# Expert sums: a 0/1 scatter in the rounded format, the gate moved to VectorE, the additions spread over four steps

## The chip, the cores and the metric

One core of one Trainium2 chip runs the whole program. The metric is the device time of one execution in microseconds; a kernel's time is the median of its runs.

## What is computed

The program runs two model blocks one after the other. The change touches only the last part of the second one, the mixture of eight experts over 256 tokens, each of 1024 features:

```python
def moe_swiglu(x, w_router, w_gu, w_down):
    logits = jnp.einsum('bsd,de->bse', x, w_router).astype(jnp.float32)
    top_logits, top_idx = lax.top_k(logits, TOP_K)
    top_gates = jax.nn.softmax(top_logits, axis=-1)
    gates = jnp.sum(jax.nn.one_hot(top_idx, N_EXPERTS, dtype=jnp.float32) * top_gates[..., None], axis=-2)
    gates = gates.astype(x.dtype)
    out = jnp.zeros_like(x)
    for e in range(N_EXPERTS):
        out = out + gates[..., e:e + 1] * swiglu_2(x, w_gu[e], w_down[e])
    return out
```

`swiglu_2` is `silu(x·Wg) * (x·Wu)`, then a product with `w_down`; the hidden width is 2816. All arrays are float32.

## The kernel before

**Products in the rounded format.** TensorE takes float32 operands in a rounded format (F32R). To keep the precision, every weight tile and every input is split into a rounded high part and a low part (the value less its high part), and three products are summed: high by high, high by low, low by high. ScalarE (ACT) writes the high parts (`w_hi`, `x_hi`, `k_hi`), VectorE (DVE) subtracts and writes the low parts (`w_lo`, `x_lo`, `k_lo`). There is one `w_hi`/`w_lo` buffer for each of three kinds of weight tile: front, back and down. So the high part of the next back tile can only be written after the matmuls of the current back tile have read it.

**An expert.** For each expert at most 128 of the 256 tokens are gathered by matmuls with a 0/1 matrix (`gather`, L1036) into `x_hi`/`x_lo`. They fill columns 0 to 127 of each 256-wide tile; columns 128 to 255 are free in this stage. The hidden width is walked in 11 steps of 256. Step p of TensorE does four things in this order: `front` (12 matmuls of 512 columns, the first half of the features, L1059), `turn_hidden` (two transposes of the hidden tile of step p-1, L1073), `back` (12 matmuls, the other half of the features, L1059), and `down` (12 matmuls that add the hidden tile of step p-1, times its part of `w_down`, to PS banks 0 and 1, L1084 to L1086). The down of an expert's last hidden tile therefore stands in step 0 of the next expert.

**The other engines in a step.** ACT: `hidden_high` (k_hi of the turned tile, L1535), `high("front")`, `silu` (L1531), `high("back")`, `high("down")` (all three at L1526). DVE: `hidden_low` (L2260, k_lo, which the down of that step waits for), `low("front")`, `hidden` (L2256, the product of gate and up), `low("back")`, `low("down")` (all three at L2250). Each of these waits for what it reads, and an engine takes them strictly in the order written. SyncE issues the weight loads, three tiles ahead of use for each kind.

**The sum of an expert.** When the last down of an expert is done, its output y (128 tokens by 1024) stands in banks 0 and 1. ACT copies it to `y_exp` in step 0 (`y_copy`, L1540). In step 1 TensorE, after its front, multiplies it by the scatter matrix: four float32 products of 512 columns into banks 2, 3, 7 and 5 (`scatter_sum`, L1094). It then clears banks 0 and 1 (`zero_sum`, L1049). The matrix holds the gate of each token, and zeros; DVE makes it in `make_picks` (L2238), TensorE turns it (`turn_scatter`), ACT copies it (`scatter_copy`, L1519). DVE adds the four banks to `moe_sum`, which lies in U: bank 5 in step 1 after `hidden_low`, the other three at the end of step 1 (`add`, L2265). TensorE's down of step 1 waits for bank 5's addition.

**The order** is written by hand, in one program for each engine, with counting semaphores. The loop over experts runs seven times; the first expert's beginning and the last expert's end stand outside it. The program makes one pass over the experts here.

Of the kernel before, what the change touches and what calls it, by code (L numbers as in the profile page):

```python
# [18 lines left out]
F32 = mybir.dt.float32  # L19
# [52 lines left out]
B_WO2 = B_Q + 4  # L72
B_MOE = B_WO2 + 4
assert B_FFN % RING == 0
MOE_SLOTS = [(B_MOE + i) % RING for i in range(3)]
ROWS2 = 18

# [46 lines left out]
def causal_mask():  # L124
# [8 lines left out]
        "raw_c": 16, "hi_ready": 3, "silu_done": 2, "dve_step": 2},  # L133
    "expert": {
        "front_ready": 11, "back_ready": 11, "down_ready": 11, "x_ready": 2, "staged": 11, "hidden_ready": 11,
        "sum_added": 2, "picked": 1, "y_copied": 1, "scatter_ready": 1, "down_used": 11, "gathered": 1,
        "front_used": 11, "back_used": 11, "hidden_turned": 11, "scatter_turned": 1, "scattered": 1, "raw_a":
        128, "raw_b": 64, "raw_c": 128, "front_in_1": 128, "back_in_1": 128, "front_in_2": 96, "back_in_2": 96,
        "down_in_1": 64, "down_in_2": 48, "hi_ready": 33, "xh_ready": 2, "moe_silu": 11, "kh_ready": 11,
        "dve_step": 1},  # L140
    "pass": {
        "front_ready": 88, "back_ready": 88, "down_ready": 88, "x_ready": 16, "staged": 88, "hidden_ready": 88,
        "sum_added": 16, "picked": 9, "y_copied": 8, "scatter_ready": 8, "down_used": 88, "gathered": 8,
        "front_used": 88, "back_used": 88, "hidden_turned": 88, "scatter_turned": 8, "scattered": 8, "raw_a":
        1024, "raw_b": 512, "raw_c": 1024, "front_in_1": 1024, "back_in_1": 1024, "front_in_2": 768,
        "back_in_2": 768, "down_in_1": 512, "down_in_2": 384, "hi_ready": 264, "xh_ready": 16, "moe_silu": 88,
        "kh_ready": 88, "dve_step": 10},
    "layer": {
        "weights_ready": 123, "gains_in": 160, "prm_ready": 1, "scaled_ready": 6, "x_ready": 14, "staged": 76,
        "s5_ready": 1, "s5c_ready": 1, "c_ready": 8, "b_ready": 8, "c_evicted": 41, "cv_ready": 8, "in_ready":  # L150
# [82 lines left out]
def build(nc, a, out):  # L233

    ctx = ExitStack()
    with ctx:
# [78 lines left out]
        n_pass = work[:, 7460:7461]  # L315
        cur = work[:, 7464:7470]
        pick = wk(4096, 4, P)
        scatter = wk(4608, T)
        y_exp = wk(5120, 2 * 512)
        moe_sum = flat(U5[:, :, :]).rearrange("p (t n) -> p t n", t=2)  # L320
        v_all = XC[:, 14:20, :].rearrange("p (t k) n -> p t (k n)", t=2)

# [42 lines left out]
                 "group_sq group_sum group_root group_ready acc_read glu_ready "  # L365
                 "params2_in mem_in centered att_scores att_max att_exp att_norm att_turned att_copied att_out att_evicted "
                 "rope_ang rope_table rope_psum roped mixed logits gate_diff route_exp masks_ready ranks routed "
                 "picked gathered scattered scatter_turned scatter_ready hidden_ready hidden_turned kh_ready y_copied sum_added mean_sum "
                 "z_tanh moe_silu front_in_1 back_in_1 down_in_1 front_in_2 back_in_2 down_in_2 front_ready back_ready down_ready front_used back_used down_used "
                 "act_step dve_step pool_step pool_waited sp_waited out_sent").split()  # L370
        s = {n: ctx.enter_context(nc.semaphore(n)) for n in names}
# [232 lines left out]
        def _(pe):  # L604
# [483 lines left out]

            def scatter_sum():

                pe.wait_ge(s["y_copied"], n.due("y_copied"))
                pe.wait_ge(s["scatter_ready"], n.due("scatter_ready"))
                for bank, t, b in ((2, 0, 0), (3, 0, 1), (7, 1, 0), (5, 1, 1)):
                    last = mm(PS[:, bank, :], scatter[:, t * P:(t + 1) * P], y_exp[:, 512 * b:512 * (b + 1)],  # L1094
                              start=True, stop=True, skip_group_check=True)
                last.then_inc(s["scattered"], n.one("scattered"))

            def step(gathers=False, turns=False, scatters=False):

                pe.wait_ge(s["hidden_ready"], n.due("hidden_ready"))  # L1100
                front()
                if scatters:
                    scatter_sum()
                    zero_sum()
                turn_hidden()
                if turns:
                    turn_scatter()
                if gathers:
                    gather()
                back()  # L1110
                if scatters:
                    pe.wait_ge(s["sum_added"], n.due("sum_added"))
                down()

            pe.sem_inc(s["down_used"], 1)
# [3 lines left out]
            n.due("hidden_ready")  # L1119
            pe.wait_ge(s["weights_ready"], n.due("weights_ready", 2))  # L1120
            with n.loop(pe, passes, "pass"):
                pe.wait_ge(s["sum_added"], n.due("sum_added"))
                gather(turned=False)
                zero_sum()
                pe.wait_ge(s["x_ready"], n.due("x_ready", 2))
                front()
                back()
                step()
                with n.loop(pe, N_EXPERTS - 1, "expert"):
                    with n.loop(pe, STEPS - 3, "moe_step"):  # L1130
                        step()
                    step(turns=True, gathers=True)
                    pe.wait_ge(s["x_ready"], n.due("x_ready", 2))
                    step()
# [10 lines left out]
        def _(act):  # L1145
# [391 lines left out]

            def y_copy():
                act.wait_ge(s["down_used"], n.peek("down_used"))
                fn(y_exp, PS[:, 0:2, :].rearrange("p b n -> p (b n)"), ACT.Copy).then_inc(s["y_copied"], n.one("y_copied"))  # L1540

            def step(j, inputs=False, turns=False, copies=False):

# [35 lines left out]
        def _(dve):  # L1579
# [648 lines left out]
            def make_picks(e, following=None):  # L2228

                if following is not None:  # L2230
                    v.tensor_copy(cur[:, 0:2, None], slot_of[:, :, following])
                v.tensor_copy(cur[:, 2:4, None], slot_of[:, :, e])
                then(v.tensor_copy(cur[:, 4:6, None], gate_of[:, :, e]))
                if following is not None:
                    dve.wait_ge(s["gathered"], n.due("gathered"))
                    gather_pick()
                for t in range(2):
                    ins = ts(pick[:, 2 + t, :], cst("iota", P, 0, P), cur[:, 2 + t:3 + t], cur[:, 4 + t:5 + t], EQ, MULT)  # L2238
                ins.then_inc(s["picked"], n.one("picked"))

            def expert_inputs():
# [18 lines left out]
                tt(k_lo[:, 0:2, 0:P], PS[:, 6, 0:T].rearrange("p (k n) -> p k n", n=P),  # L2260
                   k_hi[:, 0:2, 0:P].bitcast(F32), SUB).then_inc(s["staged"], n.one("staged"))

            def add(t, b, bank):
                part = moe_sum[:, t, 512 * b:512 * (b + 1)]
                return tt(part, part, PS[:, bank, :], ADD)  # L2265

            def add_bank_5():
                dve.wait_ge(s["scattered"], n.due("scattered"))
                add(1, 1, 5).then_inc(s["sum_added"], n.one("sum_added"))

            def add_rest():
                for t, b, bank in ((0, 0, 2), (0, 1, 3), (1, 0, 7)):
                    ins = add(t, b, bank)
                ins.then_inc(s["sum_added"], n.one("sum_added"))

            def step(j, inputs=False, adds=False):

                hidden_low()
                if adds:
                    add_bank_5()  # L2280
                low("front", (j + 1) % STEPS)
                if inputs:
                    expert_inputs()
                hidden()
                low("back", (j + 1) % STEPS)
                low("down", j)
                if adds:
                    add_rest()

            dve.sem_inc(s["sum_added"], 2)  # L2290
            n.given["sum_added"] += 2
            dve.sem_inc(s["hidden_ready"], 1)
            n.given["hidden_ready"] += 1
            for kind, count in (("front", 3), ("back", 3), ("down", 2)):
# [2 lines left out]
            with n.loop(dve, passes, "pass"):  # L2297
                first_pick()
                low("down", 0)
                expert_inputs()  # L2300
                low("front", 1)
                hidden()
                low("back", 1)
                step(1)
                with n.loop(dve, N_EXPERTS - 1, "expert") as e:
                    for j in range(2, STEPS - 1):
                        step(j)
                        if j == 7:
                            make_picks(bass.ds(e, 1), bass.ds(e + 1, 1))
                    step(STEPS - 1, inputs=True)  # L2310
                    step(0)
                    step(1, adds=True)
                for j in range(2, STEPS - 1):
                    step(j)
                    if j == 7:
                        make_picks(slice(N_EXPERTS - 1, N_EXPERTS))
                step(STEPS - 1)
                n.due("gathered")
                hidden_low()
                add_bank_5()  # L2320
                add_rest()
                dve.wait_ge(s["sum_added"], n.last("sum_added"))
                then(ts(slot_of, slot_of, -float(SLOTS), None, ADD))
            layer_norm(moe_sum, split=False)
# [52 lines left out]
```

## Time and profile before

| what | value |
|---|---|
| median of three runs | 3215.32 us (3211.72 to 3215.64) |
| the profiled execution | 3210.52 us |
| its span | 3208.7 us |
| mean granted TensorE clock | 0.955 of full speed |
| TensorE matmul busy | 2953.6 us, 92% of the span |
| VectorE busy | 2233.0 us, 70% |
| ScalarE busy | 1673.4 us, 52% |
| expert stage | from about 2350 us to the end |

The shares are averages over very different stages. A matmul's record is longer than its turn on the engine, since the next one starts while it drains; the pace of TensorE is read from starts, not from durations. Idle time is shown in square brackets behind an instruction, with what ended it.

### The profile page before, as it was taken

To read this page: it belongs to the slowest core of one execution; us is meant where nothing else is said; L and a number is where in the kernel's file an instruction comes from. 1 tells how busy PE (TensorE), PEld (TensorE's weight loads), DVE (VectorE), ACT (ScalarE), POOL (GpSimd) and SP (SyncE) were. 2 spreads that over 40 slices of the span, in tenths; PEclk is the share of its full clock that TensorE was granted. 3 is DMA by queue.
4 is the path that set the end of the run, shared out by engine and by line. 5 is a ranking of instruction groups with operands and counts; after the bars stand their busy time and mean duration, and the time that the engine had idled before them with its cause. 6 is when DMAs were issued, how large, how long until landed. Compare 5 with 4: busy or idle time off the path is not lost.

```text
span 3208.7 us, 51731 instructions
## 1 busy us (share of the span) xinstructions
PE 2953.6 (92%) x20597; PEld 2645.5 (82%) x20597; DVE 2233.0 (70%) x2614; ACT 1673.4 (52%) x1838; POOL 74.2 (2%) x68
## 2 busy tenths in 40 slices
PE   8988899989989988898989998998679999999997
PEld 7988898979989888888879896998467877787775
DVE  5778975655556779857555554555658888888887
ACT  4444566334444444563344443444446776677665
POOL 0000013000000000030000000000000000000000
PEclk9998999999999988999999998999879999999999
DMA  7553342446545533433545453555079999999995
GB/s 238 167 155 105 93 139 86 158 143 199 177 156 185 177 105 94 119 118 108 176 156 196 159 183 118 178 176 171 14 262 328 344 336 342 328 327 343 351 327 191
DMA packets 488733, 619.87 MB, mean 193 GB/s; under 512 B 34689, under 2 KB 439059, under 8 KB 488595
## 3 DMA queue, kind: packets, MB, share of 16 engines
q1 hardware_dynamic: 488595, 617.91, 58.3%
q8 instruction: 101, 1.65, 0.2%
q14 instruction: 37, 0.30, 0.0%
HBM read 616.81 MB, written 1.05 MB: 193 GB/s over the span
## 4 chain that ended last, share of the span: by engine, by line
PE 77%; DVE 14%; ACT 5%; issue 3%; DMA 0%; DVEq 0%; SPq 0%; ACTq 0%
PE PS L1059 13%; PE PS L612 12%; PE PS L613 12%; PE PS L614 12%; PE PS L665 12%; DVE w_lo L1594 3%; PE PS L1084 3%; PE PS L1086 3%; PE PS L1085 3%; ACT w_hi L1157 2%; ACT w_hi L1526 1%; PE PS L1094 1%; PE PS L794 1%; PE PS L1036 1%; PE PS L756 1%
## 5 line engine op out<-in xcount | busy, mean ns | idle before, releaser
L612 PE MATMUL PS<-x_hi,w_hi 128*128 128x256 f32 x3360 | 976.4, 291 | 11.5 <-DVE x_lo L2061 7.1
L613 PE MATMUL PS<-x_hi,w_lo 128*128 128x256 f32 x3360 | 966.8, 288 | 0.0
L614 PE MATMUL PS<-x_lo,w_hi 128*128 128x256 f32 x3360 | 965.5, 287 | 0.0
L1594 DVE TENSOR_TENSOR w_lo<-raw,w_hi 128x2048 fp32r<-128x2048 f32 x313 | 711.6, 2288 | 330.7 <-ACT w_hi L1157 330.0
L1157 ACT ACTIVATE w_hi<-raw 128x2048 fp32r<-128x2048 f32 x313 | 598.6, 1913 | 397.4 <-PE PS L665 248.0
L612 PEld LDWEIGHTS PS<-x_hi,w_hi 128*128 128x128 f32 x3360 | 662.1, 197 | 23.3 <-issue 12.0
L613 PEld LDWEIGHTS PS<-x_hi,w_lo 128*128 128x128 f32 x3360 | 662.4, 197 | 1.9
L614 PEld LDWEIGHTS PS<-x_lo,w_hi 128*128 128x128 f32 x3360 | 661.3, 197 | 0.0
L1059 PE MATMUL PS<-w_hi,x_hi 128*128 128x512 f32 x704 | 285.3, 405 | 9.5 <-DVE x_lo L2244 6.7
L1059 PE MATMUL PS<-w_lo,x_hi 128*128 128x512 f32 x704 | 276.7, 393 | 0.0
L1059 PE MATMUL PS<-w_hi,x_lo 128*128 128x512 f32 x704 | 275.3, 391 | 0.0
L2250 DVE TENSOR_TENSOR w_lo<-raw,w_hi 128x2048 fp32r<-128x2048 f32 x96 | 219.7, 2288 | 40.2 <-ACT w_hi L1526 39.8
L1659 DVE TENSOR_TENSOR k_hi<-act_out,PS 128x256 fp32r<-128x256 f32 x110 | 46.3, 420 | 279.4 <-PE PS L614 277.6
L2250 DVE TENSOR_TENSOR w_lo<-XC,w_hi 128x2048 fp32r<-128x2048 f32 x88 | 201.7, 2292 | 41.6 <-ACT w_hi L1526 41.4
L665 PE MATMUL PS<-w_hi,k_hi 128*128 128x512 f32 x568 | 179.9, 398 | 15.2 <-DVE k_lo L1952 13.6
L1526 ACT ACTIVATE w_hi<-raw 128x2048 fp32r<-128x2048 f32 x96 | 183.8, 1915 | 14.0 <-PE PS L1086 14.0
L665 PE MATMUL PS<-w_lo,k_hi 128*128 128x512 f32 x568 | 177.6, 394 | 0.0
L665 PE MATMUL PS<-w_hi,k_lo 128*128 128x512 f32 x568 | 177.1, 393 | 0.0
L1526 ACT ACTIVATE w_hi<-XC 128x2048 fp32r<-128x2048 f32 x88 | 168.3, 1912 | 8.3 <-PE PS L1059 8.3
L1211 ACT ACTIVATE act_out<-PS 128x256 f32<-128x256 f32 x55 | 21.1, 383 | 280.2 <-PE PS L614 280.2
L1059 PEld LDWEIGHTS PS<-w_hi,x_hi 128*128 128x128 f32 x704 | 132.9, 189 | 38.4 <-issue 10.9
L1059 PEld LDWEIGHTS PS<-w_lo,x_hi 128*128 128x128 f32 x704 | 132.7, 188 | 29.7
(401 smaller groups left out, 4491.7 us busy)
## 6 DMA issues: line engine op xcount, KB each, us to landing
XC<-in_w_gu_moe_dram SPq DMA_DIRECT2D x176, 512.0 KB, 8.8
raw<-in_w_gu_moe_dram SPq DMA_DIRECT2D x132, 512.0 KB, 7.9
raw<-in_w_in_dram SPq DMA_DIRECT2D x64, 1024.0 KB, 5.7
raw<-in_ffn_w_gate_dram SPq DMA_DIRECT2D x44, 1024.0 KB, 5.3
raw<-in_ffn_w_up_dram SPq DMA_DIRECT2D x44, 1024.0 KB, 6.8
raw<-in_ffn_w_down_dram SPq DMA_DIRECT2D x44, 1024.0 KB, 5.0
raw<-in_w_down_moe_dram SPq DMA_DIRECT2D x32, 1024.0 KB, 10.1
G<-in_w_down_moe_dram SPq DMA_DIRECT2D x32, 1024.0 KB, 9.5
```

What stands on the lines that cost most here:

```text
L612: mm(dst, w_hi[:, slot, w0:w0 + P], hi, start=start, stop=False, skip_group_check=True)
L613: mm(dst, w_lo[:, slot, w0:w0 + P], hi, start=False, stop=False, skip_group_check=True)
L614: return mm(dst, w_hi[:, slot, w0:w0 + P], lo, start=False, stop=True, skip_group_check=True)
L665: last = mm(PS[:, bank + 2 * t + b, :], left, right[:, slot, kt * D + 512 * b:kt * D + 512 * (b + 1)], start=False, stop=True, skip_group_ ...
L1059: last = mm(PS[:, 4, :], left, right, start=(k0 + k == 0 and right is whi and left is hi), stop=True, skip_group_check=True)
L1084: mm(PS[:, b, :], hi, whi, start=False, stop=True, skip_group_check=True)
L1085: mm(PS[:, b, :], lo, whi, start=False, stop=True, skip_group_check=True)
L1086: last = mm(PS[:, b, :], hi, wlo, start=False, stop=True, skip_group_check=True)
L1157: fn(w_hi[:, slot, :], raw[:, slot, :], ACT.Copy).then_inc(s["hi_ready"], n.one("hi_ready"))
L1526: fn(w_hi[:, MOE_SLOT[kind], :], MOE_RAW[kind][j % 3], ACT.Copy).then_inc(s["hi_ready"], n.one("hi_ready"))
L1594: tt(w_lo[:, slot, :], raw[:, slot, :], w_hi[:, slot, :].bitcast(F32), SUB)\
L2250: tt(w_lo[:, slot, :], MOE_RAW[kind][j % 3], w_hi[:, slot, :].bitcast(F32), SUB)\
```

## The change

- The scatter matrix holds ones and zeros, without the gates. It is copied to `k_hi[:, 2, :]`, in the rounded format.
- y is split as other operands are: ACT writes the high part to `x_hi[:, :, 128:256]` in step 0, and DVE writes the low part to `x_lo[:, :, 128:256]` in a new function `y_low`, in step 1 after `low("back")`.
- `scatter_sum` is eight products in the rounded format (high and low for each of four banks), in place of four in float32. It waits for `y_low`. Together with `zero_sum` it stands after the back of step 1, ahead of the down.
- DVE multiplies by the gate where it adds (`scalar_tensor_tensor`), one bank at the end of each of steps 1 to 4, in the order 5, 2, 3, 7. The wait ahead of the down of step 1 is gone.

```diff
-                pe.wait_ge(s["y_copied"], n.due("y_copied"))
+                pe.wait_ge(s["y_split"], n.due("y_split"))
                 pe.wait_ge(s["scatter_ready"], n.due("scatter_ready"))
-                for bank, t, b in ((2, 0, 0), (3, 0, 1), (7, 1, 0), (5, 1, 1)):
-                    last = mm(PS[:, bank, :], scatter[:, t * P:(t + 1) * P], y_exp[:, 512 * b:512 * (b + 1)],
-                              start=True, stop=True, skip_group_check=True)
+                for bank, t, b in SUMS:
+                    for part, y in enumerate((y_hi, y_lo)):
+                        last = mm(PS[:, bank, :].rearrange("p (k n) -> p k n", k=4), scatter[:, t * P:(t + 1) * P],
+                                  y[:, 4 * b:4 * b + 4, :], start=(part == 0), stop=(part == 1), skip_group_check=True)
                 last.then_inc(s["scattered"], n.one("scattered"))
...
                 front()
-                if scatters:
-                    scatter_sum()
-                    zero_sum()
                 turn_hidden()
...
                 back()
                 if scatters:
-                    pe.wait_ge(s["sum_added"], n.due("sum_added"))
+                    scatter_sum()
+                    zero_sum()
                 down()
...
-                fn(y_exp, PS[:, 0:2, :].rearrange("p b n -> p (b n)"), ACT.Copy).then_inc(s["y_copied"], n.one("y_copied"))
+                fn(y_hi, PS[:, 0:2, :].rearrange("p b (k n) -> p (b k) n", n=P), ACT.Copy).then_inc(s["y_copied"], n.one("y_copied"))
...
-                    ins = ts(pick[:, 2 + t, :], cst("iota", P, 0, P), cur[:, 2 + t:3 + t], cur[:, 4 + t:5 + t], EQ, MULT)
+                    ins = ts(pick[:, 2 + t, :], cst("iota", P, 0, P), cur[:, 2 + t:3 + t], None, EQ)
...
+            def y_low():
+                dve.wait_ge(s["y_copied"], n.due("y_copied"))
+                tt(y_lo, PS[:, 0:2, :].rearrange("p b (k n) -> p (b k) n", n=P), y_hi.bitcast(F32), SUB)\
+                    .then_inc(s["y_split"], n.one("y_split"))
...
+                ins = stt(part, PS[:, bank, :], cur[:, 4 + t:5 + t], part, MULT, ADD)
...
                 hidden_low()
-                if adds:
-                    add_bank_5()
                 low("front", (j + 1) % STEPS)
                 if inputs:
                     expert_inputs()
                 hidden()
                 low("back", (j + 1) % STEPS)
+                if splits:
+                    y_low()
                 low("down", j)
-                if adds:
-                    add_rest()
+                if adds is not None:
+                    add(adds)
```

The order of DVE's instructions in step 1 of an expert and at the start of step 2, before (ISA rows are waits; L2250 are the low parts of front, back and down, L2256 is `hidden`, L2265 the additions):

```order
L2260 TENSOR_TENSOR k_lo<-PS,k_hi 128x2x128
L2265 TENSOR_TENSOR U<-U,PS 128x512
L2249 ISA
L2250 TENSOR_TENSOR w_lo<-XC,w_hi 128x2048
L2254 ISA
L2256 TENSOR_TENSOR stage<-act_out,PS 128x256
L2249 ISA
L2250 TENSOR_TENSOR w_lo<-G,w_hi 128x2048
L2249 ISA
L2250 TENSOR_TENSOR w_lo<-G,w_hi 128x2048
L2265 TENSOR_TENSOR U<-U,PS 128x512 x3
```

And the same step now (L2265 is `y_low` here, L2273 an addition):

```order
L2260 TENSOR_TENSOR k_lo<-PS,k_hi 128x2x128
L2249 ISA
L2250 TENSOR_TENSOR w_lo<-XC,w_hi 128x2048
L2254 ISA
L2256 TENSOR_TENSOR stage<-act_out,PS 128x256
L2249 ISA
L2250 TENSOR_TENSOR w_lo<-G,w_hi 128x2048
L2265 TENSOR_TENSOR x_lo<-PS,x_hi 128x8x128
L2249 ISA
L2250 TENSOR_TENSOR w_lo<-G,w_hi 128x2048
L2273 SCALAR_TENSOR_TENSOR U<-PS,work,U 128x512
L2260 TENSOR_TENSOR k_lo<-PS,k_hi 128x2x128
```

The additions left their two places; one stands at the end of this step, and the other three at the ends of the next three. `y_low` stands third from the end, behind the low part of the back tile.

TensorE, end of the front of step 1 to the start of its back, before (L1094 the scatter, L1049 `zero_sum`, L1073 `turn_hidden`):

```order
L1059 MATMUL PS<-w_lo,x_hi 128x512
L1091 ISA
L1094 MATMUL PS<-work 128x512 x4
L1049 MATMUL PS<-zero_bf 128x512 x2
L1073 MATMUL PS<-con,stage 128x128 x2
L1059 MATMUL PS<-w_hi,x_hi 128x512
```

Now, from the end of the back of step 1 to the start of its down (L1096 the scatter, L1050 `zero_sum`):

```order
L1060 MATMUL PS<-w_lo,x_hi 128x512
L1096 MATMUL PS<-x_hi,k_hi 128x512
L1096 MATMUL PS<-x_lo,k_hi 128x512
L1096 MATMUL PS<-x_hi,k_hi 128x512
L1096 MATMUL PS<-x_lo,k_hi 128x512
L1096 MATMUL PS<-x_hi,k_hi 128x512
L1096 MATMUL PS<-x_lo,k_hi 128x512
L1096 MATMUL PS<-x_hi,k_hi 128x512
L1096 MATMUL PS<-x_lo,k_hi 128x512
L1050 MATMUL PS<-zero_bf 128x512 x2
L1080 ISA
L1085 MATMUL PS<-w_hi,k_hi 128x512
```

The scatter moved behind twelve matmuls and two transposes, to the place just ahead of the down.

## Rows read from the trace of the kernel before

**Rows 1.** Windows of the expert stage: busy by engine, PEclk, DMA share, GB/s

```profile
2480.00:2560.00 80.00, 78.76 (x371) 64.73 (x370) 72.05 (x56) 57.40 (x46) 0.00 (x0) 1.00 1.01 343
```

**Rows 2.** Waits, 2380 to 3200 us: total us, times, longest

```profile
ACT w_hi L1526 <- PE PS L1086: 55.8, 73, 1.7
PE PS L1084 <- DVE k_lo L2260: 13.2, 15, 4.5
```

**Rows 3.** Timeline of TensorE in an ordinary step (start, us, engine, line)

```profile
2424.07 0.39 PE L1059 MATMUL PS<-w_hi,x_hi 128*128 128x512 f32 x1
...
2426.79 0.38 PE L1073 MATMUL PS<-con,stage 128*128 128x128 f32 x2
...
2429.78 0.39 PE L1084 MATMUL PS<-w_hi,k_hi 128*128 128x512 f32 x1
...
2432.50 0.39 PE L1059 MATMUL PS<-w_hi,x_hi 128*128 128x512 f32 x1
```

**Rows 4.** The scatter line's matmuls in the whole trace

```profile
L1094 PE MATMUL PS<-work x64: 591/592/697, 2473.9 to 3192.7; 128*128 128x512 f32 x64
```

**Rows 5.** Timeline of TensorE, step 1 of the second expert and step 2

```profile
2471.22 0.39 PE L1059 MATMUL PS<-w_hi,x_hi 128*128 128x512 f32 x1
...
2473.93 3.59 PE L1094 MATMUL PS<-work 128*128 128x512 f32 x8
...
2483.75 0.39 PE L1059 MATMUL PS<-w_hi,x_hi 128*128 128x512 f32 x1
...
2490.43 0.50 PE L1084 MATMUL PS<-w_hi,k_hi 128*128 128x512 f32 x1 [0.81 <-DVE k_lo L2260]
...
2493.33 0.39 PE L1059 MATMUL PS<-w_hi,x_hi 128*128 128x512 f32 x1
```

**Rows 6.** Timeline of ACT and DVE in the ordinary step

```profile
2428.49 0.42 DVE L2260 TENSOR_TENSOR k_lo<-PS,k_hi 128x256 fp32r<-128x256 f32 x1
...
2430.26 1.92 ACT L1526 ACTIVATE w_hi<-G 128x2048 fp32r<-128x2048 f32 x1
...
2431.64 0.41 DVE L2256 TENSOR_TENSOR stage<-act_out,PS 128x256 f32<-128x256 f32 x1
...
2432.21 2.29 DVE L2250 TENSOR_TENSOR w_lo<-G,w_hi 128x2048 fp32r<-128x2048 f32 x1
```

**Rows 7.** Timeline of DVE at the end of step 1

```profile
2488.17 1.88 DVE L2265 TENSOR_TENSOR U<-U,PS 128x512 f32<-128x512 f32 x3
2489.97 0.41 DVE L2260 TENSOR_TENSOR k_lo<-PS,k_hi 128x256 fp32r<-128x256 f32 x1
```

**Rows 8.** Groups of DVE by form: count, busy us, mean ns

```profile
L2265 DVE TENSOR_TENSOR U<-U,PS 128x512 f32<-128x512 f32 x32 | 20.3, 679 | 9.5 <-PE PS L1094 9.5
L1626 DVE SCALAR_TENSOR_TENSOR x_lo<-PS,prm,x_hi 128x256 fp32r<-128x256 f32 x48 | 19.3, 476 | 13.6 <-ACT x_hi L1191 13.6
L2244 DVE TENSOR_TENSOR x_lo<-PS,x_hi 128x512 fp32r<-128x512 f32 x16 | 10.3, 685 | 20.6 <-ACT x_hi L1514 20.6
...
L2238 DVE TENSOR_SCALAR work<-con,work 128x128 f32<-128x128 f32 x16 | 4.8, 340 | 0.0
L2220 DVE TENSOR_SCALAR work<-con,work 128x128 f32<-128x128 f32 x16 | 3.9, 283 | 1.5 <-DVE work L2233 1.4
```

**Rows 9.** Timeline of TensorE after two idle stretches, then two windows (PEclk third from the end)

```profile
2362.97 0.79 PE L1059 MATMUL PS<-w_hi,x_hi 128*128 128x512 f32 x1 [6.73 <-DVE x_lo L2244]
...
3183.84 0.53 PE L1084 MATMUL PS<-w_hi,k_hi 128*128 128x512 f32 x1 [4.50 <-DVE k_lo L2260]
...
2363.00:2368.20 5.20, 5.20 (x12) 4.10 (x13) 0.00 (x0) 0.00 (x0) 0.00 (x0) 0.50 1.09 367
...
3184.00:3187.50 3.50, 3.50 (x9) 2.76 (x10) 0.00 (x0) 0.00 (x0) 0.00 (x0) 0.53 0.00 0
```

**Rows 10.** Timeline after the last down: ACT's copy and DVE's additions

```profile
3188.47 1.02 ACT L1540 ACTIVATE work<-PS 128x1024 f32<-128x1024 f32 x1 [7.07 <-PE PS L1086]
...
3193.29 2.48 DVE L2265 TENSOR_TENSOR U<-U,PS 128x512 f32<-128x512 f32 x4 [9.50 <-PE PS L1094]
```

More of the change, by code:

```diff
@@ L74 @@
 assert B_FFN % RING == 0
+SUMS = ((5, 1, 1), (2, 0, 0), (3, 0, 1), (7, 1, 0))
 MOE_SLOTS = [(B_MOE + i) % RING for i in range(3)]
@@ L135 @@
         "front_ready": 11, "back_ready": 11, "down_ready": 11, "x_ready": 2, "staged": 11, "hidden_ready": 11,
-        "sum_added": 2, "picked": 1, "y_copied": 1, "scatter_ready": 1, "down_used": 11, "gathered": 1,
+        "sum_added": 1, "picked": 1, "y_split": 1, "scatter_ready": 1, "down_used": 11, "gathered": 1,
         "front_used": 11, "back_used": 11, "hidden_turned": 11, "scatter_turned": 1, "scattered": 1, "raw_a":
@@ L139 @@
         "down_in_1": 64, "down_in_2": 48, "hi_ready": 33, "xh_ready": 2, "moe_silu": 11, "kh_ready": 11,
-        "dve_step": 1},
+        "y_copied": 1, "dve_step": 1},
     "pass": {
         "front_ready": 88, "back_ready": 88, "down_ready": 88, "x_ready": 16, "staged": 88, "hidden_ready": 88,
-        "sum_added": 16, "picked": 9, "y_copied": 8, "scatter_ready": 8, "down_used": 88, "gathered": 8,
+        "sum_added": 8, "picked": 9, "y_split": 8, "scatter_ready": 8, "down_used": 88, "gathered": 8,
         "front_used": 88, "back_used": 88, "hidden_turned": 88, "scatter_turned": 8, "scattered": 8, "raw_a":
@@ L146 @@
         "back_in_2": 768, "down_in_1": 512, "down_in_2": 384, "hi_ready": 264, "xh_ready": 16, "moe_silu": 88,
-        "kh_ready": 88, "dve_step": 10},
+        "kh_ready": 88, "y_copied": 8, "dve_step": 10},
     "layer": {
@@ L317, in build @@
         pick = wk(4096, 4, P)
-        scatter = wk(4608, T)
-        y_exp = wk(5120, 2 * 512)
+        scatter = k_hi[:, 2, :]
+        y_hi, y_lo = x_hi[:, :, P:T], x_lo[:, :, P:T]
         moe_sum = flat(U5[:, :, :]).rearrange("p (t n) -> p t n", t=2)
@@ L367, in build @@
                  "rope_ang rope_table rope_psum roped mixed logits gate_diff route_exp masks_ready ranks routed "
-                 "picked gathered scattered scatter_turned scatter_ready hidden_ready hidden_turned kh_ready y_copied sum_added mean_sum "
+                 "picked gathered scattered scatter_turned scatter_ready hidden_ready hidden_turned kh_ready y_copied y_split sum_added mean_sum "
                  "z_tanh moe_silu front_in_1 back_in_1 down_in_1 front_in_2 back_in_2 down_in_2 front_ready back_ready down_ready front_used back_used down_used "
@@ L1121, in _ @@
             with n.loop(pe, passes, "pass"):
-                pe.wait_ge(s["sum_added"], n.due("sum_added"))
+                pe.wait_ge(s["sum_added"], n.peek("sum_added"))
                 gather(turned=False)
@@ L2261, in hidden_low, with add, step @@
                    k_hi[:, 0:2, 0:P].bitcast(F32), SUB).then_inc(s["staged"], n.one("staged"))
-            def add(t, b, bank):
-                part = moe_sum[:, t, 512 * b:512 * (b + 1)]
[L2265 to L2276, printed above, removed]
+            def y_low():
+                dve.wait_ge(s["y_copied"], n.due("y_copied"))
+                tt(y_lo, PS[:, 0:2, :].rearrange("p b (k n) -> p (b k) n", n=P), y_hi.bitcast(F32), SUB)\
+                    .then_inc(s["y_split"], n.one("y_split"))
+            def add(i):
+                bank, t, b = SUMS[i]
+                if i == 0:
+                    dve.wait_ge(s["scattered"], n.due("scattered"))
+                part = moe_sum[:, t, 512 * b:512 * (b + 1)]
+                ins = stt(part, PS[:, bank, :], cur[:, 4 + t:5 + t], part, MULT, ADD)
+                if i == 3:
+                    ins.then_inc(s["sum_added"], n.one("sum_added"))
+            def step(j, inputs=False, splits=False, adds=None):
                 hidden_low()
-                if adds:
-                    add_bank_5()
                 low("front", (j + 1) % STEPS)
@@ L2285, in step @@
                 low("back", (j + 1) % STEPS)
+                if splits:
+                    y_low()
                 low("down", j)
-                if adds:
-                    add_rest()
-            dve.sem_inc(s["sum_added"], 2)
-            n.given["sum_added"] += 2
+                if adds is not None:
+                    add(adds)
+            dve.sem_inc(s["sum_added"], 1)
+            n.given["sum_added"] += 1
             dve.sem_inc(s["hidden_ready"], 1)
@@ L2303, in _ @@
                 low("back", 1)
-                step(1)
+                for j in range(1, 5):
+                    step(j)
                 with n.loop(dve, N_EXPERTS - 1, "expert") as e:
-                    for j in range(2, STEPS - 1):
+                    for j in range(5, STEPS - 1):
                         step(j)
@@ L2311, in _ @@
                     step(0)
-                    step(1, adds=True)
-                for j in range(2, STEPS - 1):
+                    step(1, splits=True, adds=0)
+                    for j in range(2, 5):
+                        step(j, adds=j - 1)
+                for j in range(5, STEPS - 1):
                     step(j)
@@ L2319, in _ @@
                 hidden_low()
-                add_bank_5()
-                add_rest()
+                y_low()
+                for i in range(4):
+                    add(i)
                 dve.wait_ge(s["sum_added"], n.last("sum_added"))
```

## The prediction

> **What bounds the kernel now.** Only the expert stage changes, so I read the windows first. There TensorE is busy for 78.8 of 80 us and its granted clock is 1.00; the DMA engines are busy too, at 343 GB/s [rows 1]. Which of the two bounds is told by the waits: ACT, which takes the loaded weights, waits for TensorE (55.8 us) and not for a landing, and TensorE's own largest wait behind an engine is 13.2 us for the low part of the hidden tile [rows 2]. So the loads keep up, and the stage lasts as long as TensorE's sequence. The timeline gives its pace: twelve matmuls from 2429.78 to 2432.50, 0.227 us each, and a whole step from 2424.07 to 2432.50, 8.43 us [rows 3]. A microsecond added to or taken from TensorE in a step is one in the time, seven times (the step with the scatter stands in a loop of seven rounds; the eighth expert's sum stands behind the loop).
>
> Step 1 of an expert, with the scatter, runs from 2471.22 to 2483.75, 12.53 us, which is 4.10 more than an ordinary one. The step behind it runs to 2493.33, 9.58 us, which is 1.15 more: its down waits 0.81 us for k_lo [rows 5]. That k_lo starts at 2489.97, behind three additions of 1.88 us together [rows 7].
>
> **The scatter itself.** Before, four float32 products are 8 records in the trace of each expert [rows 4, 5] (64 for eight experts), and last 3.59 us; less the 0.16 by which a record outlasts its turn (0.39 against 0.227) that is 3.43 us, or 0.86 for one product. After, eight products in the rounded format of the same 512 columns take 8 x 0.227 = 1.82 us. Saved: 1.6 us. The clearing of banks 0 and 1 only moves with it.
> The Trainium skill, page "FP8 and Floating Point Precision", section "TensorE Precision Notes", says that a true float32 product takes four passes. By four of the 0.227 us turns a product would be 0.91 us where the row gives 0.86; by that rule the saving would be 1.8 us in place of 1.6, 1.4 us more over seven experts. The row decides.
>
> **The wait ahead of the down.** With the additions spread, the 1.15 us behind step 1 go. In their place one addition precedes k_lo in each of four steps. In an ordinary step k_lo ends at 2428.49 + 0.42 = 2428.91 [rows 6], and its down starts at 2429.78 [rows 3]: 0.87 us of room, some 0.05 of it for the hand-over. The new addition reads PSUM and takes a scalar per token. Without the scalar 512 columns take 0.68 us; with one, 256 columns take 0.476 [rows 8] against 0.42 for k_lo's 256 [rows 6]. So about 0.74 us: it fits, barely. I count 0, with 0 to 0.2 us a step as bounds (four steps, seven experts: up to 5.6 us).
>
> **The new wait, the largest term.** The scatter now waits for `y_low`, and DVE has `y_low` behind the low part of the back tile of the same step. That low part needs ACT's high part, and this one can't be written until TensorE has read the old back tile, since there is one buffer. In the ordinary step: the back's turn ends at 2429.78 [rows 3]; ACT does the silu, and starts the high part at 2430.26, for 1.92 us; DVE does `hidden` at 2431.64, then the low part from 2432.21 for 2.29, until 2434.50 [rows 6]. Behind it comes `y_low`, an operation that the trace has at half this size: 512 columns take 0.685 us [rows 8], 256 take 0.42 [rows 6], so each further 256 cost 0.265, and 1024 take 1.22. It ends at about 2435.7. TensorE, which had gone from back to down at 2429.78, now stands still for **5.9 us**. Nothing on TensorE may pass: the down is queued behind the scatter, and ACT's high part of the down tile, the next hidden tile and DVE's `low("down")` all come after that down. The loads run on and fill their three buffers, which gains nothing, as they bound nothing. That y was copied already in step 0 doesn't help, for DVE's order keeps `y_low` back. Bounds: 5.6 (operations overlap at their ends by 0.07 or so each) to 6.3.
>
> **The clock.** After an idle stretch of 4.50 us the first matmul at 3183.84 is followed by 3.5 us at a granted clock of 0.53, that is mostly 1.2 GHz; after one of 6.73 us the clock is 0.50 from 2363.0 to 2368.2 [rows 9]. Work in that time costs double: 0.47 x 3.5 = 1.65 us lost after the one, 0.5 x 5.2 = 2.6 after the other. Before, the seven rounds hold no stretch of that length. Now each holds one of 5.9 us, between the two. I take **2.2 us** each, with 0 to 2.6 as bounds.
>
> **Small things.** The matrix of ones needs one ALU step fewer: two instructions go from 0.340 us towards 0.283 [rows 8], and they stand ahead of a k_lo that is late. That is -0.1 us an expert. At the end, behind the last down, `y_low` adds 1.2 us between ACT's copy and the scatter [rows 10], the scatter saves 1.6, and four additions with a scalar cost 0.06 more each: -0.1, counted as 0. ACT's copy keeps its place and its size. SyncE's order is unchanged.
>
> **The sum.** For each of seven experts: +5.9 +2.2 -1.6 -1.15 -0.1 = +5.25 us; seven times that is +37 us. Against the profiled execution: 3210.5 + 37 = 3247.5. The median of the runs shown is 4.8 us above that execution; from it the sum would be 3252. I give **3250 us**.
>
> **Rivals.**
> 1. *The clock stays up.* The stall is there, but the matmuls before and after are dense enough that no low clock is granted. For it: the one idle stretch seen at this density was shorter and its low time was the shortest. Against: both rows show the fall. Then 7 x (5.9 - 2.85) = +21: 3232 to 3236 us.
> The Trainium skill, page "TensorE: Matmul & The Clock Gate", section "HAM oscillation — how this bites in real kernels", describes a kernel whose every idle wait throws the clock back, which speaks against this rival; rows 9 agree with it.
> 2. *The additions don't fit.* If the addition with a scalar takes 0.9 to 1.0 us, k_lo is late in four steps, and the old wait comes back in smaller pieces: up to 5.6 us more, 3255 us.
> 3. *`y_low` is done in time, and the kernel is faster.* DVE has idle moments in steps 0 and 1, and y has been in its banks since step 0. If `y_split` came before the back's end, TensorE would not stand, and 2.85 us would be gained in each expert: 3210.5 - 20 = 3190 us, with the clock untouched. It decides at a stall of 2.85 us: below that it is faster. Against it stands the order of DVE's rows: `y_low` is third from the end of step 1, behind a low part that can't start until 2.4 us after the back's end, and that alone lasts 2.29. Only if I misread which step's tile that is can this happen.
>
> **Chances.** The forecast 0.82, rival 1 0.08, rival 2 0.06, rival 3 0.04. A measurement of this kernel can tell about 0.2%, 6 us, from no change. All but rival 3 are slower by more: faster 0.04, same 0.01 (a stall near 3 us without the clock), slower 0.95. The range goes from rival 1 without the clock's fall, 3232, to the sum with a clock cost of 2.6, late additions and the median's 4.8 us: 3262.
>
> **What would show it.** Right: in each round TensorE idle for about 5.9 us ahead of L1096, released by DVE's L2265; a granted clock near 0.5 behind it; L1096 at 0.227 or 0.43 apart; no wait of the down for k_lo in steps 2 to 5; each of the seven rounds about 5 us longer. Wrong: L1096 following the back at once, or the clock at 1.00 throughout the stage, or a mean of the additions above 0.8 us with k_lo waits behind them.

## The result, and the profile after

| | before | changed |
|---|---|---|
| median | 3213.52 us (3210.54 to 3215.64, 4 runs) | 3257.84 us (3255.75 to 3261.24, 4 runs) |
| the profiled execution | 3210.52 us | 3261.24 us |
| its span | 3208.7 us | 3259.4 us |
| mean granted TensorE clock | 0.955 | 0.943 |

The changed kernel takes 1.0141 times as long, with a 95% interval from 1.0125 to 1.0158: 44 us more, where 37 were forecast, and 3258 us in all for 3250. The two profiled executions differ by 50.7 us. Of these, 4.8 us stand ahead of the expert stage, in code that the change leaves alone (its first product starts at 2367.76, before at 2362.97), and aren't the change's. So I compare rounds of the expert loop, from one scatter's start to the next, and medians of whole runs.

The expert stage in the windows of the changed kernel (columns as in [rows 1]):

```profile
2480.00:2560.00 80.00, 73.94 (x313) 58.59 (x312) 64.61 (x53) 49.74 (x41) 0.00 (x0) 0.94 0.91 310
2560.00:2640.00 80.00, 74.14 (x339) 59.81 (x338) 62.74 (x47) 51.22 (x44) 0.00 (x0) 0.96 1.01 343
```

TensorE, busy for 78.8 of 80 us before, is busy for 74; its clock is below 1.00, and the loads move less because less is asked of them. The list of waits between 2380 and 3250 us shows where it stands:

```profile
PE PS L1096 <- DVE x_lo L2265: 42.6, 8, 5.8
...
PE PS L1085 <- DVE k_lo L2260: 6.7, 8, 4.5
```

The scatter (L1096) waits for `y_low` (L2265) eight times, 5.8 us at most. The wait for k_lo, 13.2 us before [rows 2], is down to 6.7, and 4.5 of it is the one behind the loop, which was there before. The first round in the timeline of TensorE:

```profile
2481.26 0.39 PE L1060 MATMUL PS<-w_lo,x_hi 128*128 128x512 f32 x1
2487.41 0.80 PE L1096 MATMUL PS<-x_hi,k_hi 128*128 128x512 f32 x1 [5.75 <-DVE x_lo L2265]
2488.00 0.63 PE L1096 MATMUL PS<-x_lo,k_hi 128*128 128x512 f32 x1
2488.43 0.63 PE L1096 MATMUL PS<-x_hi,k_hi 128*128 128x512 f32 x1
...
2491.12 1.03 PE L1050 MATMUL PS<-zero_bf 1*128 1x512 bf16 x2
2492.08 0.80 PE L1085 MATMUL PS<-w_hi,k_hi 128*128 128x512 f32 x1
...
2495.66 0.51 PE L1087 MATMUL PS<-w_lo,k_hi 128*128 128x512 f32 x1
2496.01 0.39 PE L1085 MATMUL PS<-w_hi,k_hi 128*128 128x512 f32 x1
```

The back's last product starts at 2481.26 and its turn ends at 2481.49, so TensorE stands still for 5.92 us. The profile prints 5.75, since it counts from the end of the product's record, 0.16 us later. Then products are 0.43 us apart instead of 0.227 until about 2495.8: 8.4 us at the lower clock. DVE in the same stretch:

```profile
2481.41 2.28 DVE L2250 TENSOR_TENSOR w_lo<-XC,w_hi 128x2048 fp32r<-128x2048 f32 x1
2483.60 0.41 DVE L2256 TENSOR_TENSOR stage<-act_out,PS 128x256 f32<-128x256 f32 x1
2483.93 2.28 DVE L2250 TENSOR_TENSOR w_lo<-G,w_hi 128x2048 fp32r<-128x2048 f32 x1
2486.14 1.22 DVE L2265 TENSOR_TENSOR x_lo<-PS,x_hi 128x1024 fp32r<-128x1024 f32 x1
2498.92 2.29 DVE L2250 TENSOR_TENSOR w_lo<-G,w_hi 128x2048 fp32r<-128x2048 f32 x1 [11.56 <-ACT w_hi L1526]
2501.13 0.75 DVE L2273 SCALAR_TENSOR_TENSOR U<-PS,work,U 128x512 f32<-128x512 f32 x1
2501.79 0.42 DVE L2260 TENSOR_TENSOR k_lo<-PS,k_hi 128x256 fp32r<-128x256 f32 x1
```

That is the chain of the prediction: the back tile's low part until 2486.2, then `y_low` for 1.22 us, until 2487.36, then the scatter at 2487.41. Behind `y_low` DVE stands idle for 11.56 us, since ACT's high part waits for the delayed down. The addition with a scalar takes 0.75 us, and the k_lo behind it is in time.

In the second round full speed is back much sooner. Two windows from the first and two from the second (the granted clock is the third number from the end):

```profile
2487.40:2491.00 3.60, 3.59 (x8) 2.49 (x8) 0.00 (x0) 0.00 (x0) 0.00 (x0) 0.50 1.11 350
2491.00:2495.80 4.80, 4.80 (x12) 3.07 (x12) 0.00 (x0) 0.00 (x0) 0.00 (x0) 0.50 1.06 380
...
2597.60:2601.50 3.90, 3.89 (x9) 2.61 (x10) 0.00 (x0) 0.00 (x0) 0.00 (x0) 0.50 1.10 350
2601.50:2605.00 3.50, 3.50 (x15) 2.45 (x14) 0.00 (x0) 0.00 (x0) 0.00 (x0) 0.97 1.04 391
```

In the first the clock is at its lower level for 8.4 us, in the second for 4. So it goes on in turn, with 8.7 us in each of the later long ones; four of the seven are long. The scatters start at 2487.41, 2597.61, 2705.74, 2816.00, 2924.16, 3034.32 and 3142.49 us: rounds of 110.2, 108.1, 110.3, 108.2, 110.2 and 108.2 us. Before, the starts at 2473.93 and 3091.77 are six rounds apart, 102.97 each.

### The profile page after: what moved, and what is told of

The parts are those of the page before. It is cut to its first block, busy times and chain, and to the rows that moved or that the text cites. A ratio compares the mean times of both kernels' runs of the same rounds, so it can differ in the third digit from the quotient of the medians.

```text
span 3259.4 us, 51717 instructions
## 1 busy us (share of the span) xinstructions
PE 2965.4 (91%) x20597; PEld 2659.7 (82%) x20597; DVE 2240.6 (69%) x2622; ACT 1674.0 (51%) x1838; POOL 74.2 (2%) x68
## 3 DMA queue, kind: packets, MB, share of 16 engines
q8 instruction: 101, 1.65, 0.2%
## 4 chain that ended last, share of the span: by engine, by line
PE 77%; DVE 14%; ACT 5%; issue 3%; DMA 0%; SPq 0%; DVEq 0%; ACTq 0%
PE PS L1060 13%; PE PS L613 12%; PE PS L614 12%; PE PS L615 12%; PE PS L666 11%; PE PS L1085 3%; DVE w_lo L1594 3%; PE PS L1086 3%; PE PS L1087 3%; ACT w_hi L1157 2%; ACT w_hi L1526 1%; PE PS L1096 1%; PE PS L795 1%; PE PS L757 1%; PE PS L1037 1%
## 5 line engine op out<-in xcount | busy, mean ns | idle before, releaser
L2250 DVE TENSOR_TENSOR w_lo<-raw,w_hi 128x2048 fp32r<-128x2048 f32 x96 | 219.8, 2290 | 37.4 <-ACT w_hi L1526 35.6
L2250 DVE TENSOR_TENSOR w_lo<-XC,w_hi 128x2048 fp32r<-128x2048 f32 x88 | 201.5, 2290 | 28.2 <-ACT w_hi L1526 26.3
L2250 DVE TENSOR_TENSOR w_lo<-G,w_hi 128x2048 fp32r<-128x2048 f32 x56 | 128.3, 2291 | 81.3 <-ACT w_hi L1526 80.1
```

The lines of the kernel that those rows point to most:

```text
L2250: tt(w_lo[:, slot, :], MOE_RAW[kind][j % 3], w_hi[:, slot, :].bitcast(F32), SUB)\
```

## The experiments

All ratios are against the kernel before, run beside them. Its own median was 3211.1, 3212.8 and 3214.5 us in the three sets of runs (the first set is the first four experiments, the third the last two), so differences between medians of two sets hold some 3 us of noise. The rounds in the traces are steadier, and where both are given, the reading rests on the rounds. Each diff is against the kernel named ahead of it.

**Only the additions spread.** On the kernel before:

```diff
-                if adds:
-                    add_bank_5()
                 low("front", (j + 1) % STEPS)
...
                 low("down", j)
-                if adds:
-                    add_rest()
+                if adds is not None:
+                    add(adds)
```

> The kernel before, with its float32 scatter in its old place and the gates in the matrix; only the additions are spread over the ends of steps 1 to 4, and the wait ahead of the down of step 1 is gone. Theory (the sum of the prediction): the 1.15 us that the step behind the scatter lasted longer go in each of seven rounds, and the four additions fit: about -8 us, 3205. Rival (the additions come late, and a part of the extra time of the change is theirs): the down waits for k_lo in steps 2 to 5, and the time is at or above that of before, 3213 to 3219.

Measured: 3206.65 us, ratio 0.9983 (0.9974 to 0.9992). Its rounds are 101.8 to 101.9 us, 1.1 less than before, and no down in steps 2 to 5 waits. Seven times 1.1 is the 8 us forecast; the medians show 4.4 us. This part is a small gain of its own. The time that the change costs isn't in it.

**`y_low` earlier in step 1.** On the changed kernel:

```diff
                 hidden_low()
+                if splits:
+                    y_low()
                 low("front", (j + 1) % STEPS)
...
                 low("back", (j + 1) % STEPS)
-                if splits:
-                    y_low()
```

> The change, with y_low moved in DVE's step 1 from behind the low part of the back tile to right behind hidden_low. Theory (y_low's place makes the stall, and the stall makes the low clock): y_low can start when k_lo ends, at about the back's end; TensorE waits some 1.2 us for it instead of 5.75, the clock stays at 1.00, a round is 101.3 us, and the time is 12 us under before: 3201. Rival A (the scatter in the rounded format is slow by itself, by its weight loads or strided operands): rounds stay above 103 us. Rival B (only the clock was the matter, the stall is made up for elsewhere): above 3213.

Measured: 3205.34 us, ratio 0.9983 (0.9973 to 0.9992). The scatter's wait, in the timeline of TensorE:

```profile
2480.93 0.50 PE L1096 MATMUL PS<-x_hi,k_hi 128*128 128x512 f32 x1 [1.02 <-DVE x_lo L2265]
```

One DVE instruction moved ahead of three turns 1.4% slower into 0.2% faster. Rivals A and B fall. The clock is 1.00 in all seven rounds: this shorter standstill costs about its length and nothing behind it. The round is 101.56 us for 101.3 expected, 1.8 us over seven, and I had left out that the end of the program is 1.5 us longer (below); together they are most of the 4 us by which the total missed.

**`y_low` in step 0.** On the changed kernel:

```diff
-                    step(0)
-                    step(1, splits=True, adds=0)
+                    step(0, splits=True)
+                    step(1, adds=0)
```

> The change, with y_low in DVE's step 0, between the low parts of the back and of the down tile, where DVE waits about 1 us for ACT in any case. Theory: no wait of TensorE ahead of the scatter, eight products at 0.227 us, no late k_lo: a round of about 100.1 us, seven times 2.85 us less than before, and at the end 1.5 us more: 3195. Rival A: as above, rounds above 103 us. Rival C (a part of the 1.6 us of the scatter isn't gained, since changing its stationary matrix in the rounded format costs): 3199 to 3206.

Measured: 3193.76 us, ratio 0.9950 (0.9935 to 0.9965). The rounds are 100.2 to 100.3 us. DVE, first round:

```profile
2472.82 1.22 DVE L2265 TENSOR_TENSOR x_lo<-PS,x_hi 128x1024 fp32r<-128x1024 f32 x1
2473.97 2.29 DVE L2250 TENSOR_TENSOR w_lo<-raw,w_hi 128x2048 fp32r<-128x2048 f32 x1
...
2476.18 0.42 DVE L2260 TENSOR_TENSOR k_lo<-PS,k_hi 128x256 fp32r<-128x256 f32 x1
```

`y_low` lies where DVE waited for ACT before, so it costs next to nothing, and the scatter follows the back without a gap:

```profile
2476.38 0.39 PE L1060 MATMUL PS<-w_lo,x_hi 128*128 128x512 f32 x1
2476.61 0.39 PE L1096 MATMUL PS<-x_hi,k_hi 128*128 128x512 f32 x1
2476.83 0.39 PE L1096 MATMUL PS<-x_lo,k_hi 128*128 128x512 f32 x1
```

The eight products are 0.227 us apart. Against the run with the additions alone the round is 1.65 us shorter (101.87 less 100.22), which is the scatter's 1.6 us and the 0.1 of the simpler matrix. Rivals A and C fall. Every part of the change is a gain, but for one place in an order.

**The stall filled with work.** On the changed kernel:

```diff
                 back()
                 if scatters:
+                    for i in range(24):
+                        mm(PS[:, 2, :].rearrange("p (k n) -> p k n", k=4), x_hi[:, i % 8, 0:P], x_hi[:, 0:4, 0:P],
+                           start=True, stop=True, skip_group_check=True)
                     scatter_sum()
```

> The change, with 24 dense products of 512 columns (on the expert's inputs, into bank 2 ahead of the scatter, which overwrites them) put where TensorE stands still. They do no part of the work; they take 5.45 us of the 5.75. Theory: the stall stays as it is, but the granted clock stays at 1.00; rounds become even, 102.98 + 5.75 - 1.6 - 1.15 - 0.1 = 105.9 us instead of 108.2 and 110.2 in turn: 3257.8 - 23 = 3235. Rival (the low clock comes from what the scatter and the clearing do, not from the idle stretch): the clock still falls, 3258.

Measured: 3235.58 us, ratio 1.0079 (1.0063 to 1.0094). The filling, what is left of the wait, and the clock over that stretch:

```profile
2477.69 5.60 PE L1112 MATMUL PS<-x_hi 128*128 128x512 f32 x24
2483.61 0.50 PE L1096 MATMUL PS<-x_hi,k_hi 128*128 128x512 f32 x1 [0.31 <-DVE x_lo L2268]
```

```profile
2470.00:2500.00 30.00, 29.69 (x132) 23.54 (x131) 20.72 (x16) 17.11 (x13) 0.00 (x0) 1.00 1.05 362
```

The clock is 1.00, and the rounds are even, 106.2 to 106.3 us. Work that nobody needs makes the kernel 22.3 us faster, and this is the price of the clock. By the rounds, 110.2 and 108.15 less 106.25, it is 4.0 and 1.9 us in turn, or 3.1 as the mean of four long and three short ones; the medians give 3.2. What is left against the run with `y_low` in step 0, 6.0 us a round, is the stall itself: 5.92 us, and 0.1 because the first product behind it takes 0.33 us in place of 0.227. So the one cause has two parts, 6.0 and 3.1 us, and the second goes without the first being touched.

**Half of the stall filled**, with `range(12)` in the same place:

> The change, with 12 dense products in place of 24 ahead of the scatter (they do no part of the work): 2.7 us of the stall are filled, and TensorE still stands idle for the last 3.0 us. It tells whether the low clock hangs on the length of the idle stretch. Theory (a short idle stretch leaves the clock alone; all stretches with a fall behind them in the trace of before were 4.5 us or longer): rounds of 106.2 us as with 24 products, 3236. Rival (any standstill of a few us lets it fall): rounds of 108 us and more, 3250 to 3258.

Measured: 3255.82 us, ratio 1.0132 (1.0115 to 1.0149). The rounds are 106.24, then 109.3 to 109.5 five times. The first scatter has the full clock after 3.03 us of idle; in the second round, after the same wait, it starts at full clock too, and loses it on the way:

```profile
2591.18 0.50 PE L1096 MATMUL PS<-x_hi,k_hi 128*128 128x512 f32 x1 [3.03 <-DVE x_lo L2268]
...
2592.69 0.59 PE L1096 MATMUL PS<-x_hi,k_hi 128*128 128x512 f32 x1
2593.08 0.63 PE L1096 MATMUL PS<-x_lo,k_hi 128*128 128x512 f32 x1
```

The clock falls a little earlier in each round, 1.5 us behind the scatter's start in the second and some 0.6 in the seventh; of the four executions three took 3256 to 3257 us and one 3248.95. My theory falls, and it rested on a wrong reading besides: stretches shorter than 4.5 us did cost the clock in the trace of before. One of 2.07 us, in an earlier stage, has products 0.12 us apart ahead of it and 0.21 apart behind it; one of 3.43 us leaves them 0.12 apart:

```profile
1857.40 0.28 PE L893 MATMUL PS<-w_hi,x_lo 128*128 128x256 f32 x1
1857.52 0.28 PE L894 MATMUL PS<-w_lo,x_hi 128*128 128x256 f32 x1
1859.87 0.55 PE L612 MATMUL PS<-x_hi,w_hi 128*128 128x256 f32 x1 [2.07 <-DVE x_lo L2061]
1860.22 0.41 PE L613 MATMUL PS<-x_hi,w_lo 128*128 128x256 f32 x1
1860.43 0.41 PE L614 MATMUL PS<-x_lo,w_hi 128*128 128x256 f32 x1
...
1295.01 1.06 PE L737 MATMUL PS<-con,work 128*128 128x128 f32 x8 [3.43 <-DVE work L1844]
...
1296.03 0.28 PE L613 MATMUL PS<-x_hi,w_lo 128*128 128x256 f32 x1
1296.15 0.28 PE L614 MATMUL PS<-x_lo,w_hi 128*128 128x256 f32 x1
```

So it isn't the length alone.

**No clearing behind the scatter.** On the changed kernel:

```diff
-                        mm(PS[:, b, :], hi, whi, start=False, stop=True, skip_group_check=True)
+                        mm(PS[:, b, :], hi, whi, start=(fresh and kt == 0), stop=True, skip_group_check=True)
...
                     scatter_sum()
-                    zero_sum()
-                down()
+                down(fresh=scatters)
```

> The change, with zero_sum left out behind the scatter; the down of step 1 clears banks 0 and 1 itself, by the start flag of its first product in each bank. It asks why the low clock lasts 4.0 us in one round and 8.4 in the next. Theory A (two products of one row, with the pauses around them, are too little work for the clock to rise): without them every round has the short low time, 110.2 and 108.2 both become about 107.4, the time 3257.8 - 13 = 3245. Theory B (it hangs on when in time the stall comes): rounds still differ by 2 us or so in some order, and only the clearing's 0.5 to 1.0 us go in each: 3251 to 3254.

Measured: 3248.25 us, ratio 1.0115 (1.0098 to 1.0132). The rounds are 107.9 and 107.0 us in turn. The first one:

```profile
2487.38 0.79 PE L1096 MATMUL PS<-x_hi,k_hi 128*128 128x512 f32 x1 [5.75 <-DVE x_lo L2264]
...
2492.24 0.52 PE L1085 MATMUL PS<-w_hi,k_hi 128*128 128x512 f32 x1
2492.60 0.40 PE L1086 MATMUL PS<-w_hi,k_lo 128*128 128x512 f32 x1
2492.84 0.39 PE L1087 MATMUL PS<-w_lo,k_hi 128*128 128x512 f32 x1
```

The stall is the same, but the full pace is back at 2492.6, 5.2 us after the scatter's start, and no round has the 8.4 us: the low time is 5.2 to 5.6 and 3.1 to 3.4 us in turn. The result lies between the two theories: with the clearing the low time of every other round is over 3 us longer, and a difference of 0.95 us between the rounds remains that it doesn't explain.

**No clearing, with `y_low` in step 0:**

> y_low in DVE's step 0 as in the run split_step0, and zero_sum left out as in no_clear. Expected: rounds of 100.2 - 0.54 = 99.7 us, 3193.8 - 3.8 = 3190. If the clearing were hidden, 3194.

Measured: 3189.10 us, ratio 0.9933 (0.9917 to 0.9950); rounds of 99.4 to 99.5 us, 0.74 less than with the clearing, where 0.54 were expected. I had taken the time from the clearing's start to the next product, and not the pause ahead of it and the slower first product behind it:

```profile
2478.19 0.39 PE L1096 MATMUL PS<-x_lo,k_hi 128*128 128x512 f32 x1
2478.51 0.60 PE L1050 MATMUL PS<-zero_bf 1*128 1x512 bf16 x2
```

(These two rows are of the run with the clearing; there the products before it are 0.227 apart, and it starts 0.32 behind the last one.) With 0.74 us for the clearing, the clock's price in the run no_clear is 107.9 and 107.0 less 105.5 (106.25 of the filled run less 0.74; no run has this), 2.4 and 1.5 us, where with the clearing it is 4.0 and 1.9.

**The end kept busy as well:** 19 of the same products ahead of the last down, and 9 ahead of the last scatter.

> As step0_no_clear, and behind the loop 19 dense products where TensorE waits 4.5 us for the last k_lo, and 9 where it waits for the last y_low (they do no part of the work; bank 2 is free there). Theory: the clock is not lost ahead of the last down and in the last scatter: 1.7 us in the down and 0.8 to 1.7 in the scatter, 3187. Rival (the end is bound by DVE and ACT anyway): 3190.

Measured: 3186.26 us, ratio 0.9923 (0.9906 to 0.9939). In the run without them the last down's products come to stand 0.43 us apart, as before [rows 9]; with them they are about 0.23 us apart. Of that run, each third product:

```profile
3161.66 0.50 PE L1085 MATMUL PS<-w_hi,k_hi 128*128 128x512 f32 x1 [0.16 <-DVE k_lo L2265]
3162.46 0.40 PE L1085 MATMUL PS<-w_hi,k_hi 128*128 128x512 f32 x1
3163.15 0.40 PE L1085 MATMUL PS<-w_hi,k_hi 128*128 128x512 f32 x1
```

The gain of 2.8 us is as expected, though near what two medians of four runs can tell. This is the fastest version found, 0.8% under the kernel before.

**`y_low` done twice,** on the run with the stall filled, and with 29 filling products in place of 24:

```diff
                 if splits:
+                    dve.wait_ge(s["y_copied"], n.peek("y_copied"))
+                    tt(wk(5120, 8, P), PS[:, 0:2, :].rearrange("p b (k n) -> p (b k) n", n=P), y_hi.bitcast(F32), SUB)
                     y_low()
```

> The run filled, with y_low's subtraction done twice (first into a spare place) and 29 dense products in place of 24, so that the clock stays up. Theory (the chain from the back tile through y_low to the scatter is what TensorE waits for, one for one): rounds longer by 1.15 us (one more of 1.22, overlapping at its end), 107.4 us, and the end by 1.15: 3235.6 + 9 = 3245. Rival (something else releases the scatter, and y_low has room): 3236.

Measured: 3243.66 us, ratio 1.0098 (1.0081 to 1.0115). The rounds are 107.4 us, 1.2 more: one for one. What is added to that chain is added to the time.

**The additions in a row,** on the run with `y_low` in step 0: all four at the end of step 1.

> The run split_step0, with the four additions in one row at the end of step 1 in place of one a step. Theory (there are 0.8 us of room ahead of k_lo; additions in a row take 0.66 us each beyond the last one's overlap, 2.66 in all): k_lo is 1.9 us late in one step of each round; rounds of 102.1 us, 3193.8 + 13 = 3207. Rival (the clearing and the scatter ahead of the down give DVE more room): less than 5 us more.

Measured: 3207.57 us, ratio 0.9978 (0.9969 to 0.9988).

```profile
2492.06 2.72 DVE L2273 SCALAR_TENSOR_TENSOR U<-PS,work,U 128x512 f32<-128x512 f32 x4
2494.69 0.41 DVE L2260 TENSOR_TENSOR k_lo<-PS,k_hi 128x256 fp32r<-128x256 f32 x1
```

The down of step 2 waits 1.67 us for that k_lo, and the rounds are 102.14 us, 1.9 more. The room of 0.8 us that I read from the ordinary step is right, and the spreading is worth 13.4 us over seven rounds once the additions carry the gate (13.8 between the medians).

## Why the prediction was right, and by how much it was off

**The new wait.** Forecast 5.9 us a round from the end of the back's turn, measured 5.92 in the same way; the 5.75 that the profile prints starts later. With the slower first product behind it, which the forecast left out, it costs 6.0. That it is the order that makes it is shown by the two moves of `y_low`, and that the chain passes on one for one by the doubled one. Rival 3 was wrong in its condition: with `y_low` in time the kernel is indeed faster, by 0.5%, but the change as written doesn't have it in time. Its threshold, a stall of 2.85 us, comes out near 2.8 by the measured gains (1.1 and 1.65), but no run had a stall near it with the clock up.

**The clock.** This term was mis-sized: 2.2 us a round with 0 to 2.6 as bounds, measured 3.1, outside them. I took the two rows of before as ends, with dense work behind the idle stretch in one and in the other. The short low times, at 1.9 us, lie between these ends, and the long ones, at 4.0, above both. What stands behind it here is the scatter and the two one-row products of `zero_sum` with pauses around them. The latter have a part in the long ones, as the run without them shows (8.4 to 8.7 us with them, 5.2 to 5.6 without); the rest of the difference is open. Rival 1 (the clock stays up) fell in all seven rounds; its time, 3232 to 3236 us, is what the filled run has, 3235.58.

**The scatter.** 1.6 us saved in full, but only where the clock is up. In the changed kernel its eight products are 0.43 us apart and take as long as the four float32 ones did; I had that loss in the clock's term, not in this one. Eight products in 8 x 0.227 us hold, so the saving rests on the measured pace. The four passes that the Trainium skill (page "FP8 and Floating Point Precision", section "TensorE Precision Notes") gives a true float32 product would have made the saving 1.8; the round of the additions alone less that of `y_low` in step 0 is 1.65 with the simpler matrix in it, so the rows' 1.6 stands within 0.1.

**The additions.** The 1.15 us behind step 1 went (1.1 measured alone), and the fit was right to a few hundredths: 0.75 us measured for 0.74. Rival 2 fell.

**The simpler matrix.** The wait behind `make_picks` went from 0.43 to 0.31 us: 0.1, as forecast.

**The end.** Counted as 0, it is some 1.5 us longer: from the last down's first product to the end of the span 26.4 us for 24.9. I had the 1.2 us of `y_low` right (the idle time ahead of the last scatter goes from 1.11 to 2.37 us) and the 0.06 us for each addition. I overlooked that the clock is low there as well, so that the scatter's 1.6 us aren't saved: from its start to the additions it is 3.72 us, and before it was 3.74 (first row; the additions are in [rows 10]).

```profile
3189.55 3.70 PE L1094 MATMUL PS<-work 128*128 128x512 f32 x8 [1.11 <-ACT work L1540]
...
3239.98 0.80 PE L1096 MATMUL PS<-x_hi,k_hi 128*128 128x512 f32 x1 [2.37 <-DVE x_lo L2265]
3240.57 0.63 PE L1096 MATMUL PS<-x_lo,k_hi 128*128 128x512 f32 x1
...
3243.70 2.73 DVE L2273 SCALAR_TENSOR_TENSOR U<-PS,work,U 128x512 f32<-128x512 f32 x4 [3.78 <-PE PS L1096]
```

The sum by measured terms: 6.0 + 3.1 - 1.65 - 1.1 = 6.35 us a round (the simpler matrix stands in the 1.65), 44.4 over seven, and 1.5 at the end: 45.9. The profiled executions differ by just that from the first product of the expert stage on (50.7 less 4.8), and the medians by 44.3. Of the 9 us between that and the forecast's 37, the clock's term is 6, the end 1.5 and the slower product behind the standstill some 1.

**The range.** Its upper end, 3262 us, is 1.5 us above the sum that it names (3210.5 + 39.6 + 5.6 + 4.8 = 3260.5). The measured 3257.84 lies inside it by allowances that were made for something else, late additions that didn't come and the median's 4.8 us; the stall and the clock at their own upper bounds would have given 3253 from the profiled execution.

## What to carry to other kernels

When a product is made to wait for one more operand, look at where that operand's instruction stands in its own engine's order and what the instructions ahead of it wait for. Here it was queued behind one that could only run after TensorE had passed the point at which it then waited; the same instruction one step earlier cost next to nothing. A standstill in a dense stretch can cost more than its length, when the work behind it runs at the lower clock: here one of 5.9 us cost 3.1 more, one of about 1 us cost nothing more. The price is found by filling the standstill with products that nobody reads.

## What was not expected of the hardware

- The time at the lower clock behind the same 5.75 us of idle was 8.4 and 4 us in turn. Without the two one-row clearing products the rounds still differ, by 0.95 us instead of 2.05, and the long low time is gone. So the clearing has a part in it. What decides between the two values stays open.
- With 3.0 us of idle the clock stayed up in one round and fell in the others, in the second round 1.5 us after work had begun again. The same scatter and clearing kept 1.00 where the standstill was filled or was 1.0 us, so they don't lower the clock by themselves. It was not tried whether they, or the many zeros in the scatter's matrix, have a part in it behind a standstill.
- The loads had room left. With `y_low` in step 0 and no clearing, the window over six rounds (TensorE busy, clock, DMA share, GB/s) is

```profile
2470.00:3100.00 630.00, 627.49 (x2911) 1.00 1.03 348
```

so even at 99.5 us a round they don't bound the stage.
